# A two-block sequence model on one core: halved transforms of the long convolution, an index lookup in PSUM, and 512-column products in the feed-forward and expert up layers

## The reference, cut to what matters

```python
def conv_ffn(x, w_up, conv_w, w_down):          # block 1: 2 x 2816 up columns, causal width-3 convolution
    u = x @ w_up
    u = depthwise_conv3(u, conv_w)
    gate, val = jnp.split(u, 2, axis=-1)
    return (jax.nn.gelu(gate) * val) @ w_down

def bidirectional_fftconv(u, h_fwd, h_bwd, bias):   # block 2: long convolution over 256 tokens, 1024 channels
    kern = jnp.concatenate([h_fwd, zeros, h_bwd[1:][::-1]], axis=0)
    y = irfft(rfft(u, n=2 * L) * rfft(kern, n=2 * L), n=2 * L)[:, :L]
    return y + u * bias

def peer_ffn(xn, w_q, subkeys, u_tab, v_tab):   # 8 heads, 2 x 128 sub-keys, top 16 of 256 sums
    ...
    cand_i = i1[..., :, None] * 128 + i2[..., None, :]
    top_s, pos = lax.top_k(cand_s, 16)
    experts = jnp.take_along_axis(cand_i, pos, axis=-1)
    act = jax.nn.gelu(jnp.einsum('td,thkd->thk', xb, u[experts])) * softmax(top_s)
    return jnp.einsum('thk,thkd->td', act, v[experts])
```

## Time and profile before

| | |
|---|---|
| median of 3 runs | 1627.4 us (1626.66 to 1628.8) |
| profiled execution | 1629.26 us, span 1627.5 us |
| TensorE busy | 1581.4 us (97%), 11710 matmuls |
| GpSimd busy | 1200.9 us (74%) |
| VectorE, ScalarE busy | 970.8 us (60%), 772.6 us (47%) |
| transfers | 268 MB, mean 165 GB/s; 383 GB/s from 10 to 12 us, 370 from 4 to 6 us |
| mean granted clock of TensorE | 0.992 |

### The profile page before, as it was taken

How to read it: one execution, slowest core, us unless ns; L and a number is a source line. 1 busy time by engine, 2 the same in 40 slices (tenths; PEclk the granted TensorE clock), 3 DMA queues, 4 the chain that set the end, 5 groups by cost and what they waited for, 6 DMA issues and landing times.

```text
span 1627.5 us, 31354 instructions
## 1 busy us (share of the span) xinstructions
PE 1581.4 (97%) x11710; PEld 1434.8 (88%) x11710; DVE 970.8 (60%) x1305; ACT 772.6 (47%) x1019; POOL 1200.9 (74%) x499
## 2 busy tenths in 40 slices
PE   6999999999999999999999989999999999999997
PEld 5688799997998889989999989999998888888886
DVE  5555376756220556843149973577777999954344
ACT  4455645446554454544444444443444444444443
POOL 6643488885887755568668999777777777788984
PEclk9999999999999999999999999999999999999999
DMA  7431465554554433335545545544444454565553
GB/s 258 163 122 52 173 240 182 188 185 157 181 182 145 140 121 113 104 118 190 200 149 186 181 156 181 169 156 162 159 161 157 164 168 164 167 220 193 194 192 104
DMA packets 72628, 268.39 MB, mean 165 GB/s; under 512 B 8160, under 2 KB 8432, under 8 KB 71344
## 3 DMA queue, kind: packets, MB, share of 16 engines
q1 hardware_dynamic: 70128, 253.99, 47.2%
q0 software_dynamic: 1568, 7.64, 1.4%
q10 hardware_dynamic: 864, 5.77, 0.9%
HBM read 264.23 MB, written 3.15 MB: 164 GB/s over the span
## 4 chain that ended last, share of the span: by engine, by line
PE 35%; POOL 32%; issue 28%; ACT 1%; DMA 1%; DVE 1%; POOLq 1%; SPq 0%; DVEq 0%; ACTq 0%
PE ps L1065 34%; POOL ring_lo L1124 32%; DMA ring<-in_stream 1%; ACT ring_hi L1547 1%; PE ps L1330 0%; POOLq L1123 0%; POOLq L1131 0%; DVE big L1812 0%; PE ps L1286 0%; ACT big L1624 0%; ACT big L1626 0%; ACT big L1621 0%; DVE stat L1926 0%; ACT h_hi L1560 0%; DVE h_lo L1786 0%
## 5 line engine op out<-in xcount | busy, mean ns | idle before, releaser
L1124 POOL TENSOR_TENSOR ring_lo<-ring,ring_hi 128x1024 fp32r<-128x1024 f32 x472 | 1179.6, 2517 | 402.1 <-ACT ring_hi L1547 400.7
L1547 ACT CAST ring_hi<-ring 128x1024 fp32r<-128x1024 f32 x472 | 489.5, 1050 | 458.6 <-DMA ring<-in_stream 455.9
L1065 PE MATMUL ps<-h_hi,ring_hi 128*128 128x256 f32 x2080 | 595.1, 286 | 8.7 <-POOL ring_lo L1124 5.4
L1065 PE MATMUL ps<-h_lo,ring_hi 128*128 128x256 f32 x2080 | 589.3, 283 | 0.0
L1065 PE MATMUL ps<-h_hi,ring_lo 128*128 128x256 f32 x2080 | 589.1, 283 | 0.0
L1065 PEld LDWEIGHTS ps<-h_hi,ring_hi 128*128 128x128 f32 x2080 | 399.8, 192 | 11.8 <-issue 8.1
L1065 PEld LDWEIGHTS ps<-h_lo,ring_hi 128*128 128x128 f32 x2080 | 400.1, 192 | 0.8 <-issue 0.5
L1065 PEld LDWEIGHTS ps<-h_hi,ring_lo 128*128 128x128 f32 x2080 | 399.8, 192 | 0.0
L1065 PE MATMUL ps<-ring_hi,h_hi 128*128 128x512 f32 (+1 forms) x704 | 273.6, 389 | 14.1 <-DVE h_lo L1786 4.4
L1065 PE MATMUL ps<-ring_hi,h_lo 128*128 128x512 f32 (+1 forms) x704 | 268.5, 381 | 0.0
L1065 PE MATMUL ps<-ring_lo,h_hi 128*128 128x512 f32 (+1 forms) x704 | 268.3, 381 | 0.0
(11 more groups left out here) (298 smaller groups left out, 1526.7 us busy)
## 6 DMA issues: line engine op xcount, KB each, us to landing
ring<-in_stream SPq DMA_DIRECT2D x480, 512.0 KB, 3.7
residual<-big ACTq DMA_DIRECT2D x2, 1024.0 KB, 4.0
big<-residual ACTq DMA_DIRECT2D x2, 1024.0 KB, 5.9
x<-in_x SPq DMA_DIRECT2D x1, 1024.0 KB, 5.6
big<-in_fdecay POOLq DMA_DIRECT2D x1, 1024.0 KB, 9.6
wrow<-in_post POOLq DMA_DIRECT2D x2, 512.0 KB, 5.3
big<-in_x ACTq DMA_DIRECT2D x1, 1024.0 KB, 7.0
big<-in_dft POOLq DMA_DIRECT2D x1, 1024.0 KB, 10.5
```

Of the source, the lines that this page charges most:

```text
L1065: return nc.tensor.matmul(out, lhsT, rhs, start=start, stop=stop, skip_group_check=True)
L1124: P.tensor_tensor(ring_lo[:, h % RING, :], ring[:, h % RING, :], ring_hi[:, h % RING, :].bitcast(fp32), ALU.subtract).then_inc(S["split_lo ...
L1547: A.copy(ring_hi[:, h % RING, :], ring[:, h % RING, :]).then_inc(S["split_hi"], 1)
```

## The change

1. **Wide products.** `h_hi` and `h_lo` become two halves of one tensor `h_both`, and one matmul of 512 columns makes high weights x high tokens and high weights x low tokens side by side; low weights x high tokens (256 columns) is added to the first half. ScalarE copies the second half of the bank to SBUF, VectorE adds it to the first in PSUM. Each index takes two banks, and there are two such pairs. Used for all 22 feed-forward indices and experts 32 to 62.
2. **Feed-forward.** `ffn_up` waits from index 2 on for the whole of index i - 2 (`ffn_gated`). The Gelu of index i - 1 stands in `ffn_act` of index i, behind `ahead` in the first pairs and behind the first cast in the loop. VectorE's gated product goes to PSUM, so cast and rest read PSUM.
3. **Halved transforms.** Tokens are split into even and odd ones: each transform needs only 128 x 128 tables, 8 matmuls forward (16 before) and 32 of 128 columns back (32 of 256 before). VectorE makes sums and differences of the even and odd spectra, and again of the product's two halves. `YT` lies in PSUM.
4. **Lookup.** `EQ` lies in PSUM banks 4 to 7.
5. **Edges.** x in two transfers; GpSimd's large loads wait for the second; constants are waited for later. `centred(0)` ahead of `maxima(2)`, `KCM` in PSUM. `branch(3)` ahead of all four rests, the last `mix_transposes` ahead of the output product, one `ahead` behind the roundings. The last four halves of the experts' down layer each wait only for their own operand. The second load of tables is half as large.

```diff
-        h_hi = over_memory("h_hi", x_at, [128, KC, SEQ])
-        h_lo = sb("h_lo", [128, KC, SEQ], f32r)
+        sb("h_lo", [128, KC, SEQ], f32r)
+        h_both = over_memory("h_both", x_at, [128, 2, KC, SEQ])
+        h_hi, h_lo = h_both[:, 0], h_both[:, 1]
...
-        UR, UI, YT = Z(5, 2 * D), Z(6, 2 * D), Z(7, 2 * D)
+        UR, UI = Z(5, 2 * D), Z(6, 2 * D)
+        YT = ps[:, 4:8, :].rearrange("p a b -> p (a b)")
-        EQ = Z(15, 2048)
+        EQ = ps[:, 4:8, :].rearrange("p a b -> p (a b)")
...
                 if part:
                     pe.wait_ge(S["u_spectrum_copied"], 1)
-                for ft in range(2):
+                    pe.wait_ge(S["u_ready"], 2)
+                for odd in range(2):
                     for nh in range(2):
-                        for t in range(TOK):
-                            last = mm(ps[:, 4 + ft * 2 + nh, :], DFT[:, part * 2 + t, ft * 128:(ft + 1) * 128],
-                                      UT[:, t, nh * 512:(nh + 1) * 512], t == 0, t == 1)
+                        last = mm(ps[:, 4 + odd * 2 + nh, :], DFT[:, part * 2 + odd, :], UT[:, odd, nh * 512:(nh + 1) * 512])
...
-            pe.wait_ge(S["y_spectrum"], 2)
+            pe.wait_ge(S["y_spectrum"], 3)
             for c in range(KC):
-                for n, (y, ft) in enumerate(((YR, 0), (YR, 1), (YI, 0), (YI, 1))):
-                    last = mm(ps[:, 4 + c // 2, (c % 2) * 256:(c % 2 + 1) * 256], y[:, ft, c * 128:(c + 1) * 128],
-                              DFT[:, 4 + n, :], n == 0, n == 3)
+                for odd in range(2):
+                    first = c % 2 * 256 + odd * 128
+                    for part, y in enumerate((UR, UI)):
+                        last = mm(ps[:, 4 + c // 2, first:first + 128], y[:, odd * D + c * 128:odd * D + (c + 1) * 128],
+                                  DFT[:, 4 + 2 * part + odd, :], part == 0, part == 1)
...
+            def wide_experts(s, it=None):
+                pe.wait_ge(S["h_ready"], at(s - 1, 6, it))
+                for j in range(2):
+                    bank = 2 * (s % 2) + j
+                    w_hi, w_lo = weights(W_PEER + s, j, it, 6)
+                    for k in range(KC):
+                        mm(ps[:, bank, :], w_hi[:, tile(k)], h_both[:, :, k, :], k == 0, False)
+                        last = mm(ps[:, bank, 0:SEQ], w_lo[:, tile(k)], h_hi[:, k, :], False, k == KC - 1)
+                    multiplied(last)
...
+            def low_products(s, it=None):
+                n = W_PEER + s
+                split(2 * n + 4, it, 6)
+                if s > 32:
+                    act.wait_ge(S["columns_summed"], at(FFN_SUMS + s - 32, 6, it))
+                split(2 * n + 5, it, 6)
+                if s > 32:
+                    A.activation(H[...2 * s - 2...], ps[:, wide_banks(s - 1), 0:SEQ], ACT.Gelu_apprx_tanh).then_inc(S["h_ready"], 1)
+                act.wait_ge(S["half_multiplied"], at(2 * n + 2, 12, it))
+                A.copy(H[...2 * s...], ps[:, wide_banks(s), SEQ:2 * SEQ]).then_inc(S["low_products_copied"], 1)
...
+            for part, u in enumerate((UR, UI)):
+                dve.wait_ge(S["u_spectrum_copied"], part + 1)
+                even = flat(ps[:, 4:6, :])
+                step(V.tensor_tensor(u[:, 0:D], even, u[:, D:2 * D], ALU.add))
+                V.tensor_tensor(u[:, D:2 * D], even, u[:, D:2 * D], ALU.subtract).then_inc(S["u_ready"], 1)
...
+            for y, parts in ((YR, UR), (YI, UI)):
+                V.tensor_tensor(parts[:, 0:D], y[:, 0, :], y[:, 1, :], ALU.add)
+                last = V.tensor_tensor(parts[:, D:2 * D], y[:, 0, :], y[:, 1, :], ALU.subtract)
+            last.then_inc(S["y_spectrum"], 1)
...
             def ffn_up(i, n, it=None):
-                if i >= 4:
-                    pe.wait_ge(S["ffn_conv_dve"], at(2 * (i - 3), 8, it))
+                if i >= 2:
+                    pe.wait_ge(S["ffn_gated"], at(i - 1, 4, it))
...
             def ffn_act(i, n, it=None):
                 if it is None:
                     ahead(2 * n + 5)
+                    if i:
+                        ffn_gelu(i - 1)
                 else:
-                    for h in range(2 * n + 4 - 2 * (i % 2 == 0), 2 * n + 6):
+                    first = 2 * n + 4 - 2 * (i % 2 == 0)
+                    split(first, it, 6)
+                    ffn_gelu(i - 1, it)
+                    for h in range(first + 1, 2 * n + 6):
                         split(h, it, 6)
...
+                A.copy(CONV[:, i % 2], ps[:, wide_banks(i), SEQ:2 * SEQ]).then_inc(S["low_products_copied"], 1)
+                act.wait_ge(S["columns_summed"], at(i + 1, 4, it))
...
             def ffn_dve(i, it=None):
+                dve.wait_ge(S["low_products_copied"], at(i + 1, 4, it))
+                sums = ps[:, wide_banks(i), 0:SEQ]
+                V.tensor_tensor(sums, sums, CONV[:, i % 2], ALU.add).then_inc(S["columns_summed"], 1)
...
+                gated = ps[:, 2 * (i % 2), 0:SEQ]
+                V.tensor_tensor(gated, CONV[:, i % 2, 0, :], CONV[:, i % 2, 1, :], ALU.mult).then_inc(S["ffn_product"], 1)
...
+            sp.dma_start(x[:, 0, :], dram["x"][:, 0, :]).then_inc(S["x_loaded"], 16)
+            sp.dma_start(x[:, 1, :], dram["x"][:, 1, :]).then_inc(S["x_second_loaded"], 16)
...
+            pool.wait_ge(S["x_second_loaded"], 16)
             pool.dma_start(FW[:, 0, :], dram["fdecay"]).then_inc(S["fdecay_loaded"], 16)
```

More of the change, by code:

```diff
@@ L282, in build, with wide_banks @@
         DOWN = 2
+        FFN_SUMS = 22
+        def wide_banks(s):
+            return slice(2 * (s % 2), 2 * (s % 2) + 2)
         XR = area(0, TOK, D)
@@ L488, in gates @@
             def gates(q, it=None):
-                bank = (3 if q < 32 else 0) + q % 2
+                bank = (4 if q < 32 else 0) + q % 2
                 pe.wait_ge(S["onehots"], at(q + 1, 6, it))
@@ L538, in pe_second @@
                     down(s, it)
-            for sem in ("operand_hi", "operand_lo"):
-                pe.wait_ge(S[sem], FIRST["experts"] + 64)
             w = []
@@ L548, in pe_second @@
             for half in range(4):
+                for sem in ("operand_hi", "operand_lo"):
+                    pe.wait_ge(S[sem], FIRST["experts"] + 63 + half // 2)
                 w.append(weights(W_PEER + 126 + half // 2, half % 2))
@@ L1015, in gated, with columns @@
                 h = H[:, 64 * half:64 * half + 64, bass.ds(tok, 8)].rearrange("p j t -> p t j")
-                bank = (0 if half else 3) + q % 2
+                bank = (0 if half else 4) + q % 2
                 V.tensor_tensor(h, ps[:, bank, :].rearrange("p (t j) -> p t j", t=8), h, ALU.mult).then_inc(S["gated"], 1)
+            def columns(s, it=None):
+                dve.wait_ge(S["low_products_copied"], at(FFN_SUMS + s - 31, 6, it))
+                sums = ps[:, wide_banks(s), 0:SEQ]
+                V.tensor_tensor(sums, sums, H[:, bass.ds(at(2 * s, 12, it), 2), :], ALU.add).then_inc(S["columns_summed"], 1)
             def rest(s, it=None, span=3):
@@ L1498, in ffn_up @@
                             wait_normed(1, k)
-                        last = product(ps[:, i % 4, j * 256:(j + 1) * 256], parts(w, ALL, tile(k)),
-                                       parts(in_parts, ALL, k, ALL), k == 0, k == KC - 1)
+                        mm(ps[:, bank, :], w_hi[:, tile(k)], h_both[:, :, k, :], k == 0, False)
+                        last = mm(ps[:, bank, 0:SEQ], w_lo[:, tile(k)], h_hi[:, k, :], False, k == KC - 1)
                     multiplied(last)
@@ L1584, in norm_act @@
                         root("inv_ready", 0, 2 * k + 1, "rstd_ready")
-                    if k:
+                    if not k:
+                        act.wait_ge(S["x_second_loaded" if t else "x_loaded"], 16)
+                    else:
                         act.wait_ge(S["post_done"], (0, 0, 2)[k] + t + 1)
```

151 lines of the change are left out of this document (84 added, 67 removed).

## The result

The changed kernel takes **1603.45 us** (median of 4 runs, 1602.65 to 1604.73) against 1627.03 us, ratio 0.9855 with a 95% interval of 0.9843 to 0.9867. The forecast was 1599.6, range 1589 to 1614: right in sign and range, 3.9 us too low. The profiled execution's span is 1600.8 us (before 1627.5), and TensorE is busy 1556.4 of them.

The account below looks back on a forecast made before the run. TensorE, busy 1581 of 1627.5 us, was taken as the bound. Terms 6.5 - 2 + 7.0 + 4.1 + 4.0 + 3.1 + 0.5 + 4.6 = 27.8 us off 1627.4 gave 1599.6 us, range 1589 to 1614.

Parts of the forecast that it names:

- Experts, +6.5: Expert up layer: wide products save 0.21 us in each of 31 indices, 6.5 us, if nothing becomes late.
- Feed-forward, -2: Feed-forward: start loses 7.5 us, wide products return 4.6 and a vanished last wait 0.9; net -2 us (-8 to +2).
- the stall at product 2: Feed-forward start: up product 2 waits for all of index 0, a TensorE stall of 4.4 us (2.5 to 6.8).
- the stall at product 5: Feed-forward start: product 5 waits for Gelu 3, behind the cast of a late half, 1.4 us (0 to 3).
- Transforms, +7.0: Long convolution: halved forward transforms give 7.1 us, the inverse's 6.5 is not counted; +7.0 us (5 to 13.6).
- the two stalls for GpSimd that I had kept: Long convolution: two stalls, 2.5 us together, from GpSimd beside VectorE's products, expected to stay (0 to 5).
- Lookup, +4.1: Lookup: with comparisons in PSUM, four TensorE waits for GpSimd's low halves go, +4.1 us (2 to 4.1).
- Edges, 4.0, 3.6 and 4.6: Gains from reordering: start 4.0 us, attention 3.1 plus mix 0.5, end 4.6.
- banks binding in every pair: Rival, 17 in 100: feed-forward banks hold TensorE in every pair, 12 us over 8 pairs, ending at 1611.
- all 13.6 of the transforms: Rival, 12 in 100: the transforms give all 13.6 us if VectorE's chain runs faster while GpSimd idles, 1593.
- edges worth nothing: Rival, 6 in 100: transfers or the clock take back the 12.2 us of start, attention, mix and end, 1612.
- experts slower: Rival, 5 in 100: two bank pairs bind in the experts; at 7 us half landing, 50 us lost, 1650.

Follow-up runs that it names:

- 6.5 by the run: Changed kernel with the expert up layer alone as before (three 256-column products a tile, three banks, no copy and sum): 1609.91 us, 6.5 us slower.
- 5.5 by the run: Changed kernel with the lookup's tile of comparisons back in SBUF: 1608.93 us, ratio 0.9892, 5.5 us slower.
- three runs: Changed kernel with one part as in the kernel before: the start (1606.75 us), attention and mix (1606.46 us), or the end (1605.73 us).
- the best version: Changed kernel with wide feed-forward products only from the fifth index, convolution sums in PSUM, its result multiplied early and weights cast early: 1586.80 us.

## Why the prediction was right, point by point

- **Experts, +6.5:** right in mechanism and size; 31 x 0.20 = 6.3 by the spacing, 6.5 by the run. The two pairs of banks lost nothing: TensorE has no wait from 1000 us to the down layer at 1217.
- **Feed-forward, -2:** the sign was right, and this is the term that was mis-sized: -7.2 in the trace. First, the stall at product 2 was 6.55, not 4.4: VectorE's product waited out both GpSimd instructions, the bound of the range and not the middle that I took. Second, the half clock lasted 6 us of matmuls, 3.0 lost and not 1.7. Third, the wide products gave 0.11 us an index from the third on, some 2.6 us in all and not 4.6. With the 0.97 us at product 5 and the 0.9 us wait at the end that went: -7.5 - 3.0 + 2.6 + 0.9 = -7.0. In this profile it stayed inside -8 to +2, but not in all: the same code takes 194.1 to 195.6 us in five profiles and 199.2 to 199.6 in three, which is -10.9 to -11.3. In the three the stall at product 5 is 3.5 to 3.9 us; the forecast's range for it ended at 3.
- **Transforms, +7.0:** measured +9.7. The forward 7.1 arrived, and 2.5 more from the two stalls for GpSimd that I had kept; why they went was not tested. The inverse's 6.5 gave nothing, as said, but I had its wait in the wrong place. VectorE's chain for the products took 36.8 us (526.9 to 563.8) where I had 27 to 31, because the last four sums and differences, with both operands in SBUF, took 3.4 us each and not the 1.2 of the run with one operand in PSUM. So it ended after TensorE came (560.3): the wait of 3.5 us and 2.6 of half clock stand ahead of the inverse, and the wait of 5 us forecast for the convolution's result is not there. The chain of 26.1 us that I put in the way was real all the same; the wait only moved behind the inverse when the chain ahead was shortened.
- **Lookup, +4.1:** 4.0 in waits, 5.5 by the run.
- **Edges, 4.0, 3.6 and 4.6:** start 3.6; attention 3.0, and the mix 2.6 with the clock held and 0.8 to 1.3 without (-0.3 in one trace), for 3.1 and 0.5; end 3.8 to 4.1, the wait shorter by 2.1 us and not 2.7.
- **The sum** of 27.8 stands against 26.7 in the profiled spans and 23.6 in the medians. Part of the gap is the base: the rows were read in an execution of 1629.3 us and their sum was taken off the median of 1627.4, and the profiled execution of the changed kernel was 0.8 us under its own median. Between the two profiled executions the forecast is 1.1 us off. That is closer than the terms are, and so in part luck: the feed-forward came out 5.2 us worse than forecast, the transforms 2.7 better, and the mix 2.1 better, most of it because the clock held in that execution, which it did in three profiles of twelve.
- **The rivals:** banks binding in every pair, refuted by pairs of 11.29 us without a wait; all 13.6 of the transforms, refuted; edges worth nothing, refuted by three runs, whose ratios all lie clear of the changed kernel's; experts slower, refuted by their spacing.

What stays open: why a wide tile takes 353 ns in one stretch and 347 in another, at a granted clock of 1.00 in both. In the feed-forward it is 353 in every trace from the third index on, and 347 in the second index of the changed kernel's. In the experts it is mostly 347, but 353 or more for some indices of most traces: in the best version's, ten of the spacings are 6.44 to 6.45 us where the others are 6.34 to 6.35. From the similarities to the expert down layer the changed kernel's trace has 398.5 us, and the traces of other runs with the same code there have up to 400.2.

## What to carry to other kernels

Price a gain per instruction together with the buffers that it takes: 107 ns for 120 was worth 6.3 us where two pairs of banks sufficed, and cost 8 to 10 us where four banks had let the first indices run ahead of a chain across three engines. When a wait is removed and nothing changes, look which instruction now stands in front on the in-order engines: moving VectorE's multiplication up and ScalarE's copy of the totals down gave 6.3 us (by the ratios 6.8) that faster instructions alone had not. And before the last microseconds of a profile are explained, see whether its execution had the same clock as the others, and the kernel before the same time.

## What the runs showed of the hardware

- A VectorE product of 256 columns with both inputs in SBUF takes 0.43 us alone, and 3.77 and 4.55 when it waited out one and a half and two GpSimd instructions, though it writes PSUM. The Trainium skill (SBUF — State Buffer, "SBUF: two separate sides") says that whoever starts first holds the shared ports for its whole instruction. The trace agrees (4.55 us beside GpSimd's 4.65 for two), and shows besides that the one kept waiting was not served between GpSimd's two. That is no rule: the product of 2.29 us at 227.90 was served behind one GpSimd instruction (227.56 to 229.91), though the next began at 229.86. What decides it, no run here shows.
- Even a copy of 16 columns within SBUF took 2.32 us beside GpSimd in the lookup (L1037 at 940.72). The same page ("Who interferes with whom") lists copies among what can take the shared ports; the row agrees.
- The same wait of 2.50 us, at the same place, lowered TensorE's granted clock to the lower level in nine profiles and not in three, which moves the time by 1.3 to 1.9 us, once 2.9.
